# Prompt attention of a hybrid decoder step: query tiles in the order 0, 7, 1, 6, 2, 5, 3, 4, and one PSUM bank moved from the transposes to the output accumulators

## What is computed

```
logits = einsum('nbqgrd,nbkgd->nbgrqk', q, k) * ATT_SCALE + bias
probs, lse = _masked_softmax(logits, mask)
out = einsum('nbgrqk,nbkgd->nbqgrd', probs, v)
...
o_b = gates[..., 0:1] * o_cmp + gates[..., 1:2] * o_slc + gates[..., 2:3] * o_win
```

## Time and profile before

| what | value |
|---|---|
| median of 3 runs | 2533.23 us (2530.29 to 2534.51) |
| the profiled execution, its own time | 2533.23 us |
| its span, first to last instruction | 2531.4 us |
| mean granted TensorE clock over the span | 0.950 |
| TensorE matmul busy | 2277.5 us (90%) |
| VectorE busy | 976.4 us (39%) |
| ScalarE busy | 573.2 us (23%) |
| prompt attention, first scores to last finish | 1096.5 to 1512.1 us |

### The profile page before, as it was taken

How to read it: one execution, slowest core, us unless ns; L and a number is a source line. 1 busy time by engine, 2 the same in 40 slices (tenths; PEclk the granted TensorE clock), 3 DMA queues, 4 the chain that set the end, 5 groups by cost and what they waited for, 6 DMA issues and landing times. The chain is left out here.

```text
span 2531.4 us, 34796 instructions
## 1 busy us (share of the span) xinstructions
PE 2277.5 (90%) x13808; PEld 1475.7 (58%) x13808; DVE 976.4 (39%) x2333; ACT 573.2 (23%) x1255; POOL 464.7 (18%) x664
## 2 busy tenths in 40 slices
PE   7999998999388687658888889999999999999998
PEld 3445656666154455435555554478888888844443
DVE  3001002333033344335555652267767775600110
ACT  3000002333022233245555551111111110100110
POOL 1314212221100345100112220023223322100000
PEclk9999997999678899779999999999999999999999
DMA  7712106775566778532221413157566642510110
GB/s 240 214 73 77 47 38 231 275 273 202 149 257 247 279 286 324 194 126 79 76 76 32 140 51 105 50 167 239 200 217 200 216 145 73 176 58 1 60 36 17
DMA packets 165878, 376.31 MB, mean 149 GB/s; under 512 B 47846, under 2 KB 104526, under 8 KB 147887
## 3 DMA queue, kind: packets, MB, share of 16 engines
q1 hardware_dynamic: 131964, 148.68, 18.7%
q0 software_dynamic: 25216, 149.43, 15.3%
q10 hardware_dynamic: 8538, 75.99, 8.8%
HBM read 345.71 MB, written 99.65 MB: 176 GB/s over the span
## 5 line engine op out<-in xcount | busy, mean ns | idle before, releaser
L2669 PE MATMUL ff_ps<-ff_hx,ff_aw 128*128 128x264 f32 x2464 | 550.1, 386 | 0.9 <-DVE ff_hx L2908 0.9
L2669 PEld LDWEIGHTS ff_ps<-ff_hx,ff_aw 128*128 128x128 f32 x2464 | 467.3, 190 | 80.8 <-issue 1.2
L369 PE MATMUL in_ps<-in_w,in_xT 128*128 128x512 f32 (+1 forms) x512 | 199.6, 545 | 0.0
L795 ACT ACTIVATE pa_L<-pa_L,pa_nm 128x640 f32<-128x640 f32 (+3 forms) x192 | 142.3, 743 | 161.4 <-DVE pa_nm L831 161.2
L821 DVE CUSTOM_DVE_ANT_0 pa_L<-pa_psS,pa_T 128x512 f32<-128x512 f32 (+3 forms) x288 | 138.3, 530 | 47.5 <-PE pa_psS L672 46.4
L672 PE MATMUL pa_psS<-pa_kT,pa_qT 64*128 64x512 f32 (+3 forms) x576 | 116.2, 510 | 38.6 <-POOL pa_qT L738 35.8
L369 PEld LDWEIGHTS in_ps<-in_w,in_xT 128*128 128x128 f32 x512 | 95.2, 190 | 93.6 <-issue 84.9
L711 PE MATMUL pa_psO<-pa_PT,pa_V 128*64 128x128 f32 x1632 | 113.9, 284 | 33.8 <-DVE pa_tmp L859 14.9
L491 DVE TENSOR_SCALAR in_yout<-in_ps 128x512 f32<-128x512 f32 (+2 forms) x44 | 26.1, 593 | 300.3 <-PE in_ps L369 190.9
L690 PE MATMUL pa_psT<-pa_ident,pa_L 128*128 128x128 f32 x816 | 115.1, 281 | 22.2 <-DVE pa_PT L847 14.1
L1064 DVE COPY cmp_KT<-cmp_psT 128x512 f32<-128x512 f32 x128 | 88.6, 692 | 96.5 <-PE cmp_psT L980 94.6
(11 more groups left out here) (381 smaller groups left out, 3047.3 us busy)
## 6 DMA issues: line engine op xcount, KB each, us to landing
out_new_a_k_s<-in_cache_a_k ACTq DMA_DIRECT2D x8, 4088.0 KB
out_new_a_v_s<-in_cache_a_v ACTq DMA_DIRECT2D x8, 4088.0 KB
ff_aw<-in_w_up SPq DMA_DIRECT2D x44, 512.0 KB, 7.4
in_w<-in_w_in SPq DMA_DIRECT2D x5, 2048.0 KB, 18.4
sel_space<-in_cache_a_k SPq DMA_DIRECT2D x8, 1024.0 KB
sel_space<-in_cache_a_v SPq DMA_DIRECT2D x8, 1024.0 KB
ff_hx<-in_w_down SPq DMA_DIRECT2D x14, 512.0 KB, 4.5
sel_space<-in_cache_a_k SPq DMA_DIRECT2D x24, 256.0 KB
```

What stands on the lines that cost most here:

```text
L369: mm = pe.matmul(ps[0:n, b, 0:width], xT[:, k, t * P:t * P + n], w[:, ch % WBUF, k, 0:width], start=(k == 0), stop=(k == KC - 1))
L795: nc.scalar.activation(x, x, ACT.Exp, bias=nm[:, s, h:h + 1], scale=1.0, accum_out=sm[:, s, h:h + 1]).then_inc(s_ex, 1)
L2669: mm = pe.matmul(ps[:, bank_of(x, j, g), 0:H2], aw[:, j % 2, at, k, :], hx[:, bt, k, g * H2:g * H2 + H2], start=(k == 0), stop=(k == KH - 1))
```

## The change

It does three things in `prompt_attention`. The query tiles of every pair are taken in the order 0, 7, 1, 6, 2, 5, 3, 4 (sizes 1, 8, 2, 7, 3, 6, 4, 5; in the window kind 1, 5, 2, 5, 3, 5, 4, 5). The ring `psT` has two banks in place of three. `psO` has two banks in place of one, so `values(u)` waits for the unit two before it. The gates are placed in the free half of `psO`'s bank, and their sigmoid moves from ahead of step 11's copies to just ahead of the copy `Rs` of unit 8. Which engine copies a bank (`on_dve`) stays as it was.

```diff
 def prompt_attention(nc, io, scr, mixT, wo, cv, s_mix, s_wo, s_cvl):
     QT = SEQ // P
+    TURNS = [0, 7, 1, 6, 2, 5, 3, 4]
...
-        it, qt = u // QT, u % QT
+        it, qt = u // QT, TURNS[u % QT]
...
-        psT = m.ps("psT", [P, 3, 512])
-        psO = m.ps("psO", [P, 2, 2 * P])
+        psT = m.ps("psT", [P, 2, 512])
+        psO = m.ps("psO", [P, 2, 512])
...
-                    if b >= 3:
-                        na, nd = copied(b - 2)
-                        if on_dve(b - 3):
+                    if b >= 2:
+                        na, nd = copied(b - 1)
+                        if on_dve(b - 2):
...
-                if u:
-                    pe.wait_ge(s_wt, u)
+                if u >= 2:
+                    pe.wait_ge(s_wt, u - 1)
                 if u == QT:
                     pe.wait_ge(s_gl, 32)
-                    pe.matmul(psO[:, u % 2, 0:QT * 24], flip[:, :],
+                    pe.matmul(psO[:, u % 2, 2 * P:2 * P + QT * 24], flip[:, :],
                               gates[:, :, :].rearrange("p t n -> p (t n)"), start=True, stop=True).then_inc(s_gf, 1)
+                if u == QT + 2:
                     pe.wait_ge(s_gs, 1)
...
-                if s == QT + 3:
-                    act.wait_ge(s_gf, 1)
-                    nc.scalar.activation(gsig[:, :, :], psO[:, QT % 2, 0:QT * 24].rearrange("p (t n) -> p t n", t=QT),
-                                         ACT.Sigmoid).then_inc(s_gs, 1)
...
+                    if u == QT:
+                        act.wait_ge(s_gf, 1)
+                        nc.scalar.activation(gsig[:, :, :], psO[:, u % 2, 2 * P:2 * P + QT * 24].rearrange("p (t n) -> p t n", t=QT),
+                                             ACT.Sigmoid).then_inc(s_gs, 1)
                     nc.scalar.activation(Rs[:, u % 4, :], psO[:, u % 2, P:2 * P], ACT.Copy).then_inc(s_rs, 1)
```

More of the change, by code:

```diff
@@ L689, in transposes @@
                         j, h = x // 2, x % 2
-                        mm = pe.transpose(psT[:, b % 3, (x - x0) * P:(x - x0) * P + P],
+                        mm = pe.transpose(psT[:, b % 2, (x - x0) * P:(x - x0) * P + P],
                                           L[:, u % 3, h, j * P:j * P + P], ident[:, :])
@@ L788, in _ @@
                         act.wait_ge(s_tr, b + 1)
-                        nc.scalar.activation(PT[:, u % 3, x0:x0 + w], psT[:, b % 3, 0:w], ACT.Copy).then_inc(s_ca, 1)
+                        nc.scalar.activation(PT[:, u % 3, x0:x0 + w], psT[:, b % 2, 0:w], ACT.Copy).then_inc(s_ca, 1)
                 if s < U:
@@ L846, in copies @@
                     dve.wait_ge(s_tr, b + 1)
-                    dve.tensor_copy(PT[:, u % 3, x0:x0 + w], psT[:, b % 3, 0:w]).then_inc(s_cd, 1)
+                    dve.tensor_copy(PT[:, u % 3, x0:x0 + w], psT[:, b % 2, 0:w]).then_inc(s_cd, 1)
             def finish(u):
```

## The result

The change makes the kernel slower: **2554.43 us** (2552.15 to 2558.76, 4 runs) against 2533.87 us of the kernel before on the same chip (2530.29 to 2534.59, 4 runs), a ratio of 1.0077 with a 95% interval of 1.0052 to 1.0102, or 20.6 us. The forecast was 2540 with a range of 2524 to 2552, so the time lies above the range. It is nearly that of rival 4 (2555), which had a chance of 0.10. Slower by over 0.2% had 0.49.

A forecast was written before the change was run, and what follows sets the result against it. VectorE and ScalarE taking turns in a closed chain were taken to bound the attention stage. Stage terms summed to -1.2 us, clock falls added 8.5: 2533.2 - 1.2 + 8.5 = 2540.5, given as 2540, range 2524 to 2552.

The forecast's parts named there:

- rival 4: TensorE's clock falls at nearly all 19 new idle stretches, 1.2 us each: 2532 + 23 = 2555 us; chance 0.10.
- the clock's: TensorE's clock falls at new idle stretches as at earlier pair passages (three of six): 8.5 falls of 1.0 us, +8.5.
- The 19 idle stretches: TensorE standing 1.9 to 2.5 us before a bank until VectorE's copy: 11 in full pairs, 8 in the window kind.
- The added wait: Two-bank ring: ScalarE's copy waits for VectorE's, exponentials start 1.87 or 1.46 us late; 24.5 us over pairs 1 to 7.
- the late scores: Ahead of the unit of 8 blocks, TensorE's scores come some 0.67 us late: 4.7 us over seven pairs.
- The sum without the clock: All attention-stage terms except clock falls: -4.2 + 0.9 + 2.2 - 1.7 + 1.6 = -1.2 us against before.
- The chain and the order: Closed VectorE-ScalarE turn of 31.1 us a full pair stays; new order of units can give only 5.2 us a pair.
- The accumulators: Two accumulator banks end the values' 20.5 us of waits for a finish, but only the stage's end gains: -1.7 us.
- Rival 3: The values' wait for the accumulator is all on the path: 2533.2 - 20.5 = 2513 us; chance 0.05.
- The tail: End of the stage, where no logits are left: accumulator waits of 0.87 and 0.79 us go, -1.7 us.
- The sigmoid: Gates' sigmoid moved into the chain between exp(11) and Rs(8): table load 1.28 us plus 0.33, +1.6 us.
- The checks of the profile: Signs expected after: exponentials about 2 us after negation, L847 wait 40 us or more, no value waits, six low-clock stretches.

The follow-up runs named there:

- e10: The changed kernel once more, unaltered, against the kernel before on the same chip: 2549.77 us, ratio 1.0110.
- e9: The changed kernel plus 16 useless filling transposes on TensorE ahead of waits for VectorE's copy, from unit 1 on except unit 11: 2530.71 us, 1.0021 against before.
- e3: The changed kernel, but VectorE copies the last bank of each unit with two or more banks: 2482.51 us, 0.9842 against the kernel before.
- e1: The kernel before with only the new order of query tiles (sigmoid moved too), three transpose banks and one accumulator bank: 2516.95 us, 0.9961 against before.
- e7: New order and VectorE copying each unit's last bank, but three transpose banks and one accumulator bank as before: 2490.74 us, 0.9927 against the kernel before.
- e5: The changed kernel with VectorE copying each unit's last bank and Rs ahead of the exponentials on ScalarE: 2459.13 us, 0.9810 against the kernel before.

## Why the prediction missed

**The step that failed is the clock's: "If the clock falls at nearly half of 19, as it did at the six, that is 8.5 times" and "I take 1.0: +8.5".** The mechanism was the right one; this term of the sum was too small, in its count and in its price. The clock fell 18 times, not 8.5. The 19 idle stretches that I had counted were there, and two more in the full pairs (21 waits of 1.6 us or more for VectorE's copy); at 18 of the 21 it fell. The three where it held are the same place in three pairs, each a wait of 1.72 us, while other waits of 1.72 brought a fall. And 1.0 us was not enough for one.

Against the 414.4 us without falls, the change lost 442.4 - 414.4 = 28.0 us to its 18 falls, and in e10 436.0 - 414.4 = 21.6 us to 14: 1.5 to 1.6 us a fall, or 0.4 us for each us at the lower level. (Against the 416.0 that still hold the fillers' part it is 1.4 to 1.5, and 0.37.) The term was +8.5 and measured +28.0. That is the whole of the 19.5 us by which the stage missed (422.9 predicted, 442.4 measured), and some 9.5 of it are the count and the rest the price. The range could not hold it either: its bounds let the price go from 0.4 to 1.5 us and kept the count at 8.5.

Rival 4 had this mechanism, with 23 us, and a chance of 0.10. What I did wrong was to carry the rate at which the passages of the kernel before brought a fall over to a new kind of stretch. Two things distinguish it, and both could have been read ahead: it recurs at every large unit, and the work behind it is in the chain, so that slow transposes delay the exponentials. The second is shown above (2.26 us late with a fall, 1.80 without). That recurring is why the clock falls more often is my guess.

The Trainium skill ("TensorE: Matmul & The Clock Gate", section "A second HAM failure mode: psum-queue depth-cycling") describes a kernel that cycles through PSUM banks, leaves TensorE briefly idle between its groups, and has its clock swing between the two levels. That is what the 18 falls here look like, and e9 shows the reverse. I didn't weigh this passage in the prediction; it would have spoken for rival 4.

**The added wait: right in place and size.** Predicted were 1.87 and 1.46 us; 1.80 and 1.37 were measured at full clock. The sum over pairs 1 to 7 was 24.5 and 2.6, so 27.1; e9's by phase is 3 x 5.2 + 2 x 3.9 + 2 x 1.8 = 27.0, or some 26 without the fillers' part. By pair it lies otherwise than I had it (3.7, 3.3 and 3.3 by phase, measured 5.2, 3.3 and 1.8): the wait that belongs to the last unit of a pair is paid at the unit of 8 of the next. The sum hardly feels that. The chain of 218.0, 27.1, 4.7 for the late scores and 1.6 for the sigmoid make 251.4. e9 measured 254.2, with its fall of 2.9 and the fillers' 1.1 in it, so 250.2. The window kind was to take 124.2 and took 122.8 in e9. The sum without the clock, 414.4, is the measured 414.4. That it agrees to 0.1 us is luck, for pair 0 and the tail came out 0.7 and 1.8 us above it, and the full pairs and the window kind 1.2 and 1.4 below. In the profile of the change the check on this step (247 to 260 us from unit 8 to 64) came out wrong, 268.9, for the falls alone.

**The chain and the order: right.** 31.1 + 0.67 is e3's 31.8. (Two readings were off without effect: the 161.2 us of waits that the prediction starts from hold the 40.4 us before the stage's first negation, and the turn for three blocks adds up to 3.00, not 3.05.) Of the 36 us that the order could give at most in the full pairs, it gave 7.3 alone (254.0 to 246.7 in e1), and 5.6 in the window kind: one accumulator bank and the late scores took the rest.

**The accumulators: wrong as a rule.** I had found them worth only the tail. In the changed kernel they may be no more, as the exponentials are late anyway; no run of the change with one accumulator bank and two for the transposes shows it. With the delay gone, the second bank is worth 1.7 us a pair, 28.8 us of the stage with the falls and the unit of the sigmoid (e7 to e3). Rival 3 failed with the change as made, but its mechanism is real once the delay is gone. The Trainium skill ("PSUM — Partial Sum Buffer", Summary: rules for kernel authors) asks for a different bank when one is read while a matmul runs. It names no time. What the runs add is a condition for a gain: it shows in e7 to e3, where values wait 41.1 us for a finish.

**The tail: wrong, by a small term.** It was to be 1.7 us shorter and is 1.6 longer (11.4 for 9.7). A fall lies in it, but e9, which has none there, still takes 9.8. The exponentials of the last unit are 1.37 us late too, as it is one of the units with the added wait. The prediction counted that wait seven times in the window kind and left out the eighth, which lies in the tail. e3, without the wait, has 8.0, which is the 1.7 shorter.

**The sigmoid: right.** 1.6 us predicted. The timeline of ScalarE after:

```profile
1120.04 1.28 ACT L802 ACT_TABLE_LOAD   x1
1121.33 0.33 ACT L802 ACTIVATE pa_gsig<-pa_psO 128x192 f32<-128x192 f32 x1
1121.56 0.27 ACT L804 ACTIVATE pa_Rs<-pa_psO 128x128 f32<-128x128 f32 x1
```

Rs starts 1.52 us after the load. In e3 the same unit takes 5.48 us, and 3.84 in later pairs, 1.64 more. (All of pair 1 takes 2.4 us more than the later pairs.) The sigmoid starts 1.29 us after the load, so the further drain that the prediction weighed is not seen.

**The checks of the profile:** L793 of the unit of 7 in pair 0 started 2.0 us after its negation, TensorE's wait for VectorE's copy grew to 45.7 us, values don't wait for the finish: all three as foretold. Six falls or more: 18.

**What stays open:** why the clock fell at 18 of 21 stretches here and at 14 of the same 21 in e10, while three of the eleven TensorE waits of 1.3 us and more in the stage before brought one. The fillers show that idle time is needed for it; no experiment changed the length of a stand without changing the work around it. Also open is whether the pace of 31.8 in e5 can be passed.

**The better version.** e5, the change with the last bank copied by VectorE and Rs ahead of the exponentials, takes 2459.13 us against 2507.97, and e3 takes 2482.51 against 2529.02. Both beat both kernels: 1.9 and 1.6% under the kernel before.

## What to carry to other kernels

When a ring loses a bank, ask of each bank whose copy frees it and what stands ahead of that copy in its engine's list; here one rule of four lines for who copies which bank was worth 70 us of a stage of 442, falls included. Count the new idle stretches of TensorE and price them as if the clock fell at each, if they recur, let the count and not only the price vary in the range, and compare with a variant in which TensorE does useless work there: it separates the wait from the clock. A wait that costs nothing in the kernel as it is may be the bound of the next one, so price a part again after the delay that hides it is gone.

## What the runs showed of the hardware

The clock fell to 1.2 GHz at TensorE waits of 1.6 to 3.5 us that recur, at 18 of 21 in one execution and at 14 of the same 21 in another of the same code; with 16 useless transposes ahead of all of them but unit 11's, one fall was left. A microsecond at the lower level cost about 0.4 us here. And two executions of the same code reached attention 17 us apart, and the kernel before 26 us from the first of them (1070.5, 1087.1 and 1096.5 us), with 415 and 337 GB/s in one stretch of the gathers: a single profiled execution can hide a loss of 20 us in a stage, and the stages must be compared one by one.
